# Written-out halves, earlier splits and moved requests in a fused decoder layer

## What is computed

```python
proj = jnp.einsum('bsd,df->bsf', h, w_in)
...
y_a = jnp.einsum('bsf,fd->bsd', o_a, w_branch_attn)
y_r = jnp.einsum('bsf,fd->bsd', o_r, w_branch_ret)
merged = jax.nn.sigmoid(gate_a) * y_a + jax.nn.sigmoid(gate_b) * y_r
return jnp.einsum('bsd,de->bse', merged, w_out)
...
x = layer_norm(ALPHA * x + y, ln1_scale[l], ln1_bias[l])
y = hierarchical_moe(x, ...)
x = layer_norm(ALPHA * x + y, ln2_scale[l], ln2_bias[l])
```

## Time and profile before

| | us |
|---|---|
| median of 3 runs (2211.96 to 2212.68) | 2212.42 |
| the profiled execution, device time | 2210.98 |
| its span | 2209.1 |
| last output tile ends (T4), on its timeline | about 1197.7 |
| DMA at its full rate, experts | about 1250 to 2160 |

### The profile page before, as it was taken

How to read it: one execution, slowest core, us unless ns; L and a number is a source line. 1 busy time by engine, 2 the same in 40 slices (tenths; PEclk the granted TensorE clock), 3 DMA queues, 4 the chain that set the end, 5 groups by cost and what they waited for, 6 DMA issues and landing times.

```text
span 2209.1 us, 25383 instructions
## 1 busy us (share of the span) xinstructions
PE 2020.4 (91%) x9110; PEld 1269.8 (57%) x9110; DVE 957.3 (43%) x1257; ACT 591.8 (27%) x736; POOL 43.8 (2%) x59
## 2 busy tenths in 40 slices
PE   7999999989999999999978788988888889988885
PEld 6888888878888788878766433333333333333331
DVE  5444544544444544565534633333333332333335
ACT  4444444334444444354423200000000000000000
POOL 0000000000000000000000000000000000000000
PEclk9999999999999999999989899899999999998997
DMA  6555455455565445557385299999999999999994
GB/s 223 184 178 187 155 165 171 161 173 183 176 201 164 155 161 181 169 166 237 125 298 221 104 430 428 428 429 429 428 428 429 429 428 428 429 428 428 428 429 179
DMA packets 147303, 617.20 MB, mean 279 GB/s; under 512 B 21008, under 2 KB 21008, under 8 KB 122128
## 3 DMA queue, kind: packets, MB, share of 16 engines
q1 hardware_dynamic: 147216, 616.09, 72.5%
HBM read 613.95 MB, written 2.10 MB: 279 GB/s over the span
## 4 chain that ended last, share of the span: by engine, by line
issue 58%; PE 35%; DVE 5%; ACT 2%; DVEq 0%; POOLq 0%; POOL 0%
PE PS L784 19%; PE PS L803 12%; DVE Z L1483 3%; PE PS L821 1%; DVE SG L1453 1%; PE PS L774 1%; ACT TG L1025 1%; PE PS L792 1%; ACT HT L1027 1%; POOL RSTD L1527 0%; PE PS L737 0%; ACT ZH L1005 0%; POOLq L1526 0%; DVE HB L1455 0%; PE PS L727 0%
## 5 line engine op out<-in xcount | busy, mean ns | idle before, releaser
L424 DVE TENSOR_TENSOR WL<-RAW,WH 128x1024 fp32r<-128x1024 f32 x384 | 456.6, 1221 | 439.0 <-ACT WH L420 437.6
L435 PE MATMUL PS<-WH,XH 128*128 128x512 f32 x1216 | 485.6, 399 | 16.3 <-DVE WL L424 16.3
L437 PE MATMUL PS<-WH,XL 128*128 128x512 f32 x1216 | 475.7, 391 | 0.0
L436 PE MATMUL PS<-WL,XH 128*128 128x512 f32 x1216 | 474.9, 391 | 0.0
L420 ACT ACTIVATE WH<-RAW 128x1024 fp32r<-128x1024 f32 x384 | 393.7, 1056 | 274.7 <-PE PS L437 202.1
L784 PE MATMUL PS<-W,XE 128*64 128x512 f32 x1984 | 430.9, 592 | 0.0
L803 PE MATMUL PS<-W,HT 128*64 128x512 f32 x1024 | 290.4, 731 | 15.1 <-ACT HT L1027 15.1
L784 PEld LDWEIGHTS PS<-W,XE 128*64 128x64 f32 x1984 | 139.3, 137 | 286.4 <-issue 286.4
L435 PEld LDWEIGHTS PS<-WH,XH 128*128 128x128 f32 x1216 | 229.3, 189 | 67.0 <-DVE WL L424 22.0
L437 PEld LDWEIGHTS PS<-WH,XL 128*128 128x128 f32 x1216 | 229.0, 188 | 49.4
L436 PEld LDWEIGHTS PS<-WL,XH 128*128 128x128 f32 x1216 | 229.7, 189 | 45.3
(11 more groups left out here) (256 smaller groups left out, 1362.6 us busy)
## 6 DMA issues: line engine op xcount, KB each, us to landing
RAW<-in_w_in_dram SPq DMA_DIRECT2D x304, 512.0 KB, 4.5
W<-in_w_expert_gate_dram SPq DMA_DIRECT2D x64, 2048.0 KB, 12.7
W<-in_w_expert_up_dram SPq DMA_DIRECT2D x64, 2048.0 KB, 17.1
W<-in_w_expert_down_dram SPq DMA_DIRECT2D x64, 2048.0 KB, 12.7
RAW<-in_w_branch_ret_dram SPq DMA_DIRECT2D x32, 512.0 KB, 4.5
RAW<-in_w_out_dram SPq DMA_DIRECT2D x32, 512.0 KB, 7.9
RAW<-in_w_branch_attn_dram SPq DMA_DIRECT2D x16, 512.0 KB, 5.6
XN<-in_x_dram SPq DMA_DIRECT2D x4, 512.0 KB, 7.8
```

Of the source, the lines that this page charges most:

```text
L424: dve.tensor_tensor(WL[:, i % RING], RAW[:, i % RING], WH[:, i % RING].bitcast(F32), ALU.subtract).then_inc(lo_done, 1)
L435: pe.matmul(PS[:, bank + t], hs, wh, start=first and j == 0, stop=False)
L436: pe.matmul(PS[:, bank + t], hs, wl, start=False, stop=False)
L437: mm = pe.matmul(PS[:, bank + t], ls, wh, start=False, stop=end)
```

## The change

The hardware loop over the two halves is written out. The read of each half's last chunk moves behind the second tile of what follows (`read_chunk` at tile LAG-1). SP requests CST in two pieces (the first holds only the identity and the rotary frequencies), and x in turns with the first four weight tiles; PE transposes the first quarter of x before tile 0 and two more pairs behind each of tiles 0, 1 and 2, and the splits of x and the rotary tables are spread over tiles 0 to 8. The attention inputs of BR are split during the last four tiles of half 1, the retention inputs from branch tile 4 on. The last branch column block takes its retention tiles first. The first merged pair is split ahead of output tile 0, and the merge of column block 3 happens in DVE's work behind output tile 1. The scaling of rotated retention heads moves one tile behind the rotation. XC for column block 0 is requested behind output tile 12 instead of 6, the constants block behind tile 11 instead of 9, and expert 0's slots behind branch tiles 14 and 30 and output tiles 10, 13, 16 and 19. The banks of half 1 and of OUT change places.

```diff
+
+def pair(half, c):
+    return 2 * ((half * NC + c) % 2)
...
-ATT_AT = [65, 84, 97, 110]
+ATT_AT = [65, 86, 98, 110]
...
+NA = AW // P // KT
+
+
+def branch_tile(n):
+    j, i = divmod(n, BR_TILES)
+    if j < 3:
+        return (j, True, i) if i < NA else (j, False, i - NA)
+    return (j, False, i) if i < BR_TILES - NA else (j, True, i - BR_TILES + NA)
...
+A_END = [BR_TILES * j + NA - 1 for j in range(3)] + [BR - 1]
+R_END_AT = [BR_TILES * (j + 1) - 1 for j in range(3)] + [BR - 1 - NA]
+M_PAIRS = {-1: 0, 0: 1, 1: 2, 2: 3, 3: 4, 4: 5, 7: 6, 8: 7}
+M_READ = {6: 0, 7: 1}
...
+def out_pair(j):
+    return 2 * ((j + 1) % 2)
...
-EARLY_AT = (25,)
-EARLY_SLOTS = (2,)
...
+X_BANKS = 6
+
+X_AFTER = ((0,), (1,), (2, 3), (4, 5), (6, 7))
+
+ANGLES_AT, TRIG_AT, TABLES_AT = (4, 5, 6), 7, 8
...
+EARLY = {14: 2, 30: 0}
+LATE = {10: 1, 13: 3, 16: 4, 19: 5}
...
-        sp.dma_start(POSI[:], positions.rearrange("b (t p) -> p (b t)", p=P),
-                     allow_slow_non_contiguous=True).then_inc(pos_landed, 16)
-        sp.dma_start(CST[:], consts).then_inc(c_landed, 16)
-        for q in range(4):
+        def load_x(q):
...
-        with sp.Fori(0, 2) as half:
+        sp.dma_start(CST[:, 0:C_FIRST], consts[:, 0:C_FIRST]).then_inc(c_landed, 16)
+        for half in range(2):
...
+                    if half == 0 and c == 0:
+                        if i < 4:
+                            load_x(i)
+                        if i == 3:
+                            sp.dma_start(POSI[:], positions.rearrange("b (t p) -> p (b t)", p=P),
+                                         allow_slow_non_contiguous=True).then_inc(pos_landed, 16)
+                        if i == 5:
+                            sp.dma_start(CST[:, C_FIRST:C_END], consts[:, C_FIRST:C_END]).then_inc(m_landed, 16)
...
-            j, i = divmod(n, BR_TILES)
...
-            if n == 20:
-                sp.wait_ge(b_low, 3 * HEADS)
-            if n in EARLY_AT:
-                load_slot(0, 0, EARLY_SLOTS[EARLY_AT.index(n)])
-
-        late = [c for c in range(UNITS) if c not in EARLY_SLOTS]
+            j, a, i = branch_tile(n)
+            load_tile(sp, T2 + n, n, (w_a_k if a else w_r_k)[:, KT * i:KT * i + KT, j * CH:(j + 1) * CH])
...
+            if n in EARLY:
+                if EARLY[n] == 0:
+                    sp.wait_ge(y_read, 4)
+                else:
+                    sp.wait_ge(tile_used, T2 + RING)
+                load_slot(0, 0, EARLY[n])
...
-            if i == TPC - 2:
-                if j == 0:
-                    sp.wait_ge(m_low, KD)
...
+            if n == 12:
+                sp.wait_ge(m_low, KD)
+                sp.dma_start(XC[:], x_rows[:, :, 0:CH]).then_inc(xc_landed, 16)
...
-            if n == 9:
+            if n == 11:
...
-            if n >= 10 and n % 4 == 2 and (n - 10) // 4 < len(late):
-                load_slot(0, 0, late[(n - 10) // 4])
+            if n in LATE:
+                if n == 10:
+                    sp.wait_ge(y_read, 8)
+                load_slot(0, 0, LATE[n])
...
-        for b in range(8):
+
+        def turn_x(b):
             if b % 2 == 0:
                 pe.wait_ge(x_landed[b // 2], 16)
+            if b >= X_BANKS:
+                pe.wait_ge(x_low, b - X_BANKS + 1)
             for k in (2 * b, 2 * b + 1):
...
-        pe.wait_ge(x_low, 8)
+
+        turn_x(0)
+        turn_x(1)
...
-        with pe.Fori(0, 2) as half:
...
-                    if c == 0:
-                        pe.wait_ge(sums_read, half * NP + 1)
-                    elif c >= 2:
-                        chunk_read(half, c - 2)
-                mm = multiply_tile(pe, half * TILES + p, p, XH, XL, KT * i, 2 * (c % 2), i == 0, i == TPC - 1)
+                    if half * NC + c >= 2:
+                        chunk_read(*divmod(half * NC + c - 2, NC))
...
+                if half == 0 and p < TPC:
+                    pe.wait_ge(x_low, p + 1)
+                mm = multiply_tile(pe, half * TILES + p, p, XH, XL, KT * i, pair(half, c), i == 0, i == TPC - 1)
+                if half == 0 and p < 3:
+                    turn_x(2 * p + 2)
+                    turn_x(2 * p + 3)
...
-            j, i = divmod(n, BR_TILES)
-            if i in (0, na):
+            j, a, i = branch_tile(n)
+            if i == 0:
...
+                elif a:
+                    chunk_read(1, NC - 2)
                 else:
-                    pe.wait_ge(sums_read, 2 * NP + 1)
+                    chunk_read(1, NC - 1)
...
-        with act.Fori(0, 2) as half:
+        def branch_high(q):
+            for k in (2 * q, 2 * q + 1):
+                high, src = (OH[:, k], OT[:, k]) if k < HEADS else (RH[:, k - HEADS], RT[:, k - HEADS])
+                act.activation(high, src, ACT.Copy).then_inc(b_high, 1)
+
+        for half in range(2):
...
+                if half == 1 and p == LAG - 1:
+                    read_chunk(0, NC - 1)
+                if half == 1 and p == TILES - NA:
+                    act.wait_ge(r_done, 2 * HH)
+                    act.wait_ge(turn_read, 2 * NT + 1)
+                if half == 1 and p >= TILES - NA:
+                    branch_high(p - TILES + NA)
+                if half == 0 and p < 5:
+                    for b in X_AFTER[p]:
+                        high_x(b)
+                if half == 0 and p == TRIG_AT:
+                    act.wait_ge(red_done, 1)
+                    act.activation(TRIG[:], RED[:], ACT.Sin).then_inc(trig_done, 1)
...
-            read_chunk(half, NC - 1)
-
-
-        act.wait_ge(tile_used, T2 + RING)
-        act.wait_ge(r_read, 2 * HH)
-        act.wait_ge(turn_read, 2 * NT + 1)
...
-            if n < BR_TILES:
-                for k in (2 * n, 2 * n + 1):
-                    high, src = (OH[:, k], OT[:, k]) if k < HEADS else (RH[:, k - HEADS], RT[:, k - HEADS])
-                    act.activation(high, src, ACT.Copy).then_inc(b_high, 1)
             split_high(act, T2 + n, n, T2 // RING)
+            if n == LAG - 1:
+                read_chunk(1, NC - 1)
+                act.wait_ge(r_read, 2 * HH)
+            if NA <= n < BR_TILES:
+                branch_high(n)
...
-        act.wait_ge(tile_used, T3 + RING)
+        act.wait_ge(tile_used, T3 - NA + RING)
+        act.wait_ge(m_read, 3 * TOK)
+        merged_high(M_PAIRS[-1])
         for n in range(OUT):
-            for t in range(TOK):
...
             split_high(act, T3 + n, n, T3 // RING)
+            if n in M_READ:
+                read_merged(3, M_READ[n])
+                if M_READ[n] == TOK - 1:
+                    act.wait_ge(m_read, 4 * TOK)
+            if n in M_PAIRS:
+                merged_high(M_PAIRS[n])
...
+            if kind in ("qa", "ka"):
+                last.then_inc(rotated, 1)
+
+        def scale_heads(half, c):
+            kind = CHUNKS[c][0]
...
+                sc = CST[:, half * TOK * HH + c0:half * TOK * HH + c0 + TOK * HH].rearrange("p (t h) -> p t h", t=TOK)
+                dve.tensor_tensor(nat, nat, sc[:, :, :, None].broadcast_to((P, TOK, HH, DH)),
+                                  ALU.mult).then_inc(rotated, 1)
...
+            dve.wait_ge(m_landed, 16)
...
+                if half == 1 and p >= TILES - NA:
+                    branch_low(p - TILES + NA)
+                if half == 0 and p < 5:
+                    for b in X_AFTER[p]:
+                        low_x(b)
+                if half == 0 and p in ANGLES_AT:
+                    angles(ANGLES_AT.index(p))
+                if half == 0 and p == TABLES_AT:
+                    tables()
...
+                    if p == READ[c] + 2 and c in ROTS:
+                        scale_heads(half, c)
...
         def gate_b(j):
-            dve.wait_ge(tile_used, T2 + BR_TILES * (j + 1) + RING)
+            dve.wait_ge(tile_used, T2 + R_END_AT[j] + 1 + RING)
...
+        def merge():
             dve.drain()
             dve.tensor_tensor(NAT[:], NAT[:], TH[:], ALU.add).then_inc(m_ready, 1)
...
-        for n in range(BR + 2):
...
+        def gates_behind(n):
             for j in range(4):
-                if n == BR_TILES * j + na - 1 + LAG:
+                if n == A_END[j] + LAG:
                     gate_a(j)
-                if n == BR_TILES * (j + 1) - 1 + LAG:
+                    if j == 3:
+                        merge()
+                if n == R_END_AT[j] + LAG:
                     gate_b(j)
+                    if j < 3:
+                        merge()
...
+        for n in range(BR):
+            split_low(dve, T2 + n, n)
+            if NA <= n < BR_TILES:
+                branch_low(n)
+            gates_behind(n)
...
+        def merged_low(q):
+            for k in (2 * q, 2 * q + 1):
...
+                dve.tensor_tensor(ML[:, k], MT[:, k], MH[:, k].bitcast(F32), ALU.subtract).then_inc(m_low, 1)
+
+        merged_low(M_PAIRS[-1])
         for n in range(OUT):
...
+            if n in M_PAIRS:
+                merged_low(M_PAIRS[n])
+            gates_behind(BR + n)
```

(50 more changed lines are left out.)

124 lines of the change are left out of this document (38 added, 86 removed).

## The result

| | before | after | |
|---|---|---|---|
| median, us | 2212.19 (4 runs) | 2182.47 (4 runs) | ratio 0.9871, 95% interval 0.9859 to 0.9882 |
| profiled execution, us | 2210.98 | 2181.54 | |
| its span | 2209.1 | 2179.8 | |

The change saves 29.7 us, 1.3%. The forecast was 2178, its range 2162 to 2189. What is left to explain is 4.5 us, and where it lies.

What follows compares the result with a forecast made beforehand. PE's waits before T4 were taken as all that could be saved, the DMA bounding the experts. Gains less costs summed to 34.4 us: 2211.0 became 2176.6, and with the median 1.4 higher, 2178; range 2162 to 2189.

Steps and rivals of the forecast that it cites:

- The bound: Whole kernel: a microsecond saved before T4 is saved at the end, one for one, and nothing else can be saved.
- Start: Kernel start: tile 0 begins at 9.2 instead of 18.5 us; gain 6.3 us, bounds 4 and 7.5.
- Half seam: Between halves: written-out code and the later last-chunk read remove PE's wait and slow clock; gain 8.2 us.
- start of BR: At BR's start: inputs split beside half 1's last four tiles remove wait and slow clock; gain 6.5 us.
- start of OUT: At OUT's start: first merged pair and output tiles split ahead remove wait and slow clock; gain 6.9 us.
- thin covers: Rival: handovers between stages keep part of their waits, half the three stage-start gains stays; 2189 us, chance 0.14.
- Branch tile 36: Last branch column block: the tile writes banks gate_b(2) has yet to read; cost 1.4 us, bounds 1.2 and 2.
- The scaling: In the halves: scaling one tile later shrinks waits of 2.6 us a half to 0.6; gain 4.0, bounds 0 and 5.2.
- Output tile 10: In OUT: XC behind the constants block delays the residual and tile 10's split; PE waits 12.5 us, net loss 7.2.
- Code fetch: Rival, half 1: written-out code is fetched too slowly; at 0.3 us a tile the time is 2224, chance 0.04.
- W requests: In OUT: four weight requests instead of five, three tiles apart, remove 4.4 us of short waits; bounds 0 and 4.4.

Runs made afterwards that it cites:

- the exchanged banks: Changed kernel with the two branches' PSUM banks exchanged in the last column block, output tiles' banks back as before; single execution 2181.66 us.
- the run with the late pieces: Spread run plus expert 0's pieces of slots 1, 3, 4 and 5 (8 MB) requested behind the last output tile; 2165.80 us, ratio 0.9792.
- spread run: Changed kernel with the constants block's 15 DMAs issued one behind each of output tiles 12 to 26; 2175.18 us, ratio 0.9841.

## Why the prediction was right, and where not

**The bound.** Right. The experts kept their pace (428 GB/s), T4 moved by 30.4 us and the end by 29.3 to 29.7.

**Start.** Forecast 6.3, measured 6.4 by the twelfth turn, and that it came out so close is luck. Tile 0 started at 10.04 instead of 9.2, since x landed 0.5 us later than taken and the splits and handovers took 0.3 more. Against this, the three groups of transposes cost 2.7 us, not 3.0, and there was a gain that the sum did not have: behind the old wait at tile 0 the slow clock cost 2.3 us (granted 0.77 from 18.50 to 28.50), while the first tile of the changed kernel lost 1.7 (4.4 us instead of 2.72, with matmuls of 0.63 us each).

**Half seam, start of BR, start of OUT.** All three waits went to nothing, as costed. The seam gave 8.4 us where 8.2 stood, the start of BR 4.3 for its wait where 4.1 stood, and BR with the start of OUT 5.5 where 5.5 stood. The thin covers held.

**Branch tile 36.** Forecast 1.4, measured 1.31 as a wait and 1.6 by what the exchanged banks gave back, with the releaser named.

**The scaling.** Mis-sized: forecast 2.0 in each half, it gave 0.7 and 0.6. The step took the shift of the attention positions for harmless, though it is in the change. With the old positions 3.9 us more came, 5.2 in all, so the term itself was rather too low.

**Output tile 10.** The chain was right in each link. Its size was 12.5, measured 15.75: the block 17.7 instead of 15.6 us and XC's landing 7.2 instead of 6.1 make the 3.2. I had seen the 2 MB piece ahead of the block and put it in the bound, not in the middle; the run without it shows it worth 5 us. The sentence that the block stays long wherever it stands, and that moving it shortens nothing, was too strong: it took 15.6 us before, 17.7 behind the 2 MB piece and 12.4 without it. Only its second half kept its pace (the last four router requests in 2.8 to 2.9 us each time).

**Code fetch.** That rival fell: in half 1 PE is busy in the whole of a window at a full clock, the waits of both halves are the same to 0.02 us, and so is the time from the first turn of a chunk to the last of retention (409.25 us in each). ACT's pause of 1.80 us went with the back edge. The Trainium skill (Runtime: NRT & Kernel Launch, Instruction fetch mechanics) says that a taken branch breaks the sequential prefetch, so that a target which is not at hand has to be fetched before the engine goes on. The DMA's account agrees. It lists packets of instructions by queue (packets, MB, share), here over 18 us around the seam, from 464 us before and then from 456 us after:

```profile
q14 instruction: 6, 0.05, 0.8%
q8 instruction: 2, 0.03, 0.7%
```

```profile
q8 instruction: 1, 0.02, 0.3%
```

Eight packets have become one. No row ties a packet to ACT, so that the pause was such a fetch stays likely, not shown.

**W requests.** Forecast 4.4 us of short waits gone. They were gone in the changed kernel, but behind a hole that had filled the ring: once it was closed, 7.3 us of short waits were there again, and the run with the late pieces shows that they were the weights'. The spread run's expectation failed on this very step.

**The rest.** The sum was 34.4 us, T4 moved by 30.4. Of the 4.0 that are missing the scaling is 2.7 (4.0 forecast, 1.3 come) and OUT from its first tile 1.7; the seam and the other starts gave 0.4 more than their terms. In OUT the hole was 3.2 longer and its slow clock 0.8 cheaper, 1.7 us (0.83 of 10 us) instead of 2.5. In the other direction, the slow clock behind the old wait at tile 10 had cost about 2.8 us (granted 0.70 from 1129.80 to 1139.80, which is 3.0, less a part in which PE stood still), not 2.5. The 0.4 that are left are not settled. The cheap clock was luck: with the banks exchanged, the same wait of 15.75 us was followed by 0.76. Another 1 us is lost behind T4.

## What to carry to other kernels

When a request is moved on a queue, list all that now stands ahead of it, down to the requests that themselves wait for a backlog, and follow who waits for its landing and what stands behind that waiter; here this chain made a wait of 15.75 us. A long wait hides the shorter ones behind it (7.3 us here), so a repair is to be costed together with what it uncovers. A small shift that comes along with a change, such as two attention positions, is to be costed like the rest: it took back 3.9 us. Large transfers for a later stage belong where the DMA is idle, and that is found in a view of the DMA's rate over time, not of its mean.

## What the runs showed of the hardware

A DMA request can hold its issuing engine for long, and the price lands on one request or two: in the block, the second of eight equal router requests (1024 short runs each) took 7.75 us of SP's time with 2 MB queued ahead and 3.07 without, the others 0.66 to 0.77. A full DMA alone does not do it. In the spread kernel, with the DMA share at 1.00 from 1075 to 1130 us and an output tile between any two of them, each of the eight took 0.55 to 0.60 us. What fills up is not shown.

After a wait of 3.41 us PE's first matmul still ran at 0.47 us, and the granted clock fell only after that; over the next 10 us it was 0.83. How long PE had waited did not decide how much of the clock it lost:

| wait, us | kernel | granted clock of the next 10 us |
|---|---|---|
| 15.75 | changed | 0.83 |
| 15.75 | banks exchanged | 0.76 |
| 10.52 | no piece ahead of the block | 0.72 |
| 4.11 and 4.18 | before | 0.76 and 0.75 |
| 2.56 | spread | 1.00 |
| 2.36 | spread | 0.83 |
| 1.3, 1.5 and 1.8 | branch tile 36, the scaling, the first of spread | 1.00 |
